# Two RMS-norm roots between two fused blocks, moved from full-width rows to token columns

## The reference, cut to what matters

```
x1  = x + (1 + gt2) * conv_ffn(h, w_up, conv_w, conv_b, w_down)    # end of the first block
y   = x1 * rsqrt(mean(x1^2) + 1e-6) * g_final                      # its final norm
hn  = y  * rsqrt(mean(y^2)  + 1e-5) * norm_mix_g_2                 # first norm of the second block
u   = hn @ w_pw1 + b_pw1                                           # 2048 -> 4096
a, gate = split(u);  u = a * sigmoid(gate)                         # then a depthwise convolution of 31 taps
```

## Time and profile before

| | us |
|---|---|
| median of 3 runs | 2610.44 |
| lowest and highest of them | 2610.17, 2610.95 |
| the profiled execution, its own time | 2608.42 |
| the span of its instructions | 2606.3 |
| busy in it: PE, DVE, ACT, POOL | 2560.7, 1837.3, 1355.5, 290.4 |
| mean granted clock of TensorE, share of full speed | 0.991 |

### The profile page before, as it was taken

The page is one execution under the profiler, slowest core; times in us unless marked ns, Lnnn a source line. Parts: engine busy times, 40 slices in busy tenths (PEclk is TensorE's granted clock), DMA queues, the critical chain, the costliest instruction groups (busy, mean ns, idle before and its releaser), DMA issues. The chain is left out here.

```text
span 2606.3 us, 42280 instructions
## 1 busy us (share of the span) xinstructions
PE 2560.7 (98%) x15879; PEld 2265.6 (87%) x15879; DVE 1837.3 (70%) x2514; ACT 1355.5 (52%) x1868; POOL 290.4 (11%) x278
## 2 busy tenths in 40 slices
PE   7999999999999999999999999999999999999998
PEld 4899998888888888888888889997888888888887
DVE  3467778887888888855666657998776654566554
ACT  3445444455645555544555556997544434444443
POOL 0021122101010000000000005881000000000000
PEclk8999999999999999999999999998999999999999
DMA  9997699867786877765666565654566655666554
GB/s 367 360 306 247 205 272 295 252 203 245 234 267 213 254 245 248 236 191 187 191 187 188 191 193 147 183 174 126 180 192 187 190 190 187 190 188 189 188 185 133
DMA packets 525083, 560.68 MB, mean 215 GB/s; under 512 B 20453, under 2 KB 487841, under 8 KB 524688
## 3 DMA queue, kind: packets, MB, share of 16 engines
q1 hardware_dynamic: 504448, 487.39, 59.2%
q0 software_dynamic: 20496, 71.38, 9.0%
HBM read 553.45 MB, written 2.10 MB: 213 GB/s over the span
## 5 line engine op out<-in xcount | busy, mean ns | idle before, releaser
L836 ACT CAST whi<-raw 128x1024 fp32r<-128x1024 f32 x850 | 890.4, 1050 | 1079.8 <-PE ps L2173 905.5
L1340 DVE TENSOR_TENSOR wlo<-raw,whi 128x1024 fp32r<-128x1024 f32 x794 | 970.8, 1224 | 675.5 <-ACT whi L836 669.1
L2171 PE MATMUL ps<-xhl,whi 128*128 128x512 f32 x3584 | 1130.5, 397 | 2.1 <-DVE xhl L1418 1.8
L2173 PEld LDWEIGHTS ps<-xhl,wlo 128*128 128x128 f32 x3584 | 674.4, 188 | 159.5
L2173 PE MATMUL ps<-xhl,wlo 128*128 128x256 f32 x3584 | 705.2, 278 | 0.0
L2171 PEld LDWEIGHTS ps<-xhl,whi 128*128 128x128 f32 x3584 | 546.9, 189 | 5.5 <-issue 4.8
L2171 PE MATMUL ps<-ghl,whi 128*128 128x512 f32 x1024 | 319.5, 393 | 0.0
L2173 PEld LDWEIGHTS ps<-ghl,wlo 128*128 128x128 f32 x1024 | 192.2, 188 | 44.5
L2171 PE MATMUL ps<-fhl,whi 128*128 128x512 f32 x704 | 219.3, 392 | 0.0
L2173 PE MATMUL ps<-ghl,wlo 128*128 128x256 f32 x1024 | 202.9, 279 | 0.0
L2173 PEld LDWEIGHTS ps<-fhl,wlo 128*128 128x128 f32 x704 | 132.1, 188 | 30.6
(11 more groups left out here) (364 smaller groups left out, 2515.9 us busy)
## 6 DMA issues: line engine op xcount, KB each, us to landing
raw<-in_w_in SPq DMA_DIRECT2D x176, 512.0 KB, 4.8
raw<-in_w_up SPq DMA_DIRECT2D x176, 512.0 KB, 3.7
raw<-in_ffn_w_up SPq DMA_DIRECT2D x128, 512.0 KB, 3.7
raw<-in_ffn_w_down SPq DMA_DIRECT2D x128, 512.0 KB, 3.5
ada<-in_w_ada POOLq DMA_DIRECT2D x106, 512.0 KB, 5.0
raw<-in_w_down SPq DMA_DIRECT2D x88, 512.0 KB, 3.5
att<-in_w_ada SPq DMA_DIRECT2D x32, 1024.0 KB, 11.0
raw<-in_conv_w_pw SPq DMA_DIRECT2D x120, 256.0 KB, 3.3
```

Source lines behind the costliest of these rows:

```text
L836: nc.scalar.copy(whi[t % SPL][:, :, :], raw[t % RAW][:, :, :]).then_inc(s_hi, 1)
L1340: nc.vector.tensor_tensor(wlo[t % SPL][:, :, :], raw[t % RAW][:, :, :], whi[t % SPL][:, :, :].bitcast(F32), ALU.subtract).then_inc(s_lo, 1)
L2171: mm(o[:, m, :, :], whi[t % SPL][:, c, m * P:(m + 1) * P], x, start=first and c == 0, stop=last and c == KC - 1, skip_group_check=True)
L2173: ins = mm(o[:, m, 0, :], wlo[t % SPL][:, c, m * P:(m + 1) * P], x[:, 0, :], start=False, stop=last and c == KC - 1, skip_group_check=True)
```

## The change

The sums of squares at the seam are taken as token columns (`row_sums`), those of x1 behind the second quarter of chunk 0 as before, those of x1 * g_final behind the first products of the third quarter, into `bank_m`. DVE makes both roots on two columns, with tokens on partitions, and puts r1 and r1 * r2 on diagonals (`nwt`, `odd`). Behind the first products of the fourth quarter PE spreads them: r1 * r2 into `bank_z`, r1 and again r1 * r2 into `bank_f`. `gained_normed` reads the spread roots from `bank_z`; ACT copies the two halves of `bank_f` into `rstd` and `rstd_first`, for which `rooted` waits.

```diff
@@ ACT
             down(1)
-            root(2)
-            root(3)
-
+            root(2, slice(0, 2))
+            root(3, slice(2, 4))
+            act.wait_ge(s_statspread, 2)
+            nc.scalar.copy(rstd[:, :], bank_f[:, T:2 * T]).then_inc(s_statrows, 1)
+            nc.scalar.copy(rstd_first[:, :], bank_f[:, 0:T]).then_inc(s_statrows, 1)
@@ DVE
-            root(2, EPS1, s_var2, 3)
-            sv.did(nc.vector.tensor_copy(rstd_first[:, :], rstd[:, :]))
+            def newton(at, spare):
+
+                r, v, w = (x[:, i:i + 2] for x, i in ((rstd, at), (varr, at), (varr, spare)))
+                sv.did(nc.vector.reciprocal(r, r))
+                sv.wait()
+                sv.did(nc.vector.tensor_tensor(w, r, r, ALU.mult))
+                sv.wait()
+                sv.did(nc.vector.scalar_tensor_tensor(w, w, -0.5, v, ALU.mult, ALU.mult))
+                sv.wait()
+                sv.did(nc.vector.scalar_tensor_tensor(r, w, 1.5, r, ALU.add, ALU.mult))
+                sv.wait()
+
+            def on_diagonal(dst, roots):
+
+                for h in range(2):
+                    nc.vector.tensor_scalar(dst[:, P * h:P * (h + 1)], ident, roots[:, h:h + 1], None, ALU.mult).then_inc(s_lndiag, 1)
+
+            first_root, second_root, both = rstd[:, 0:2], rstd[:, 2:4], varr[:, 10:12]
+            squared, gained_mean = varr[:, 6:8], varr[:, 8:10]
+            dve.wait_ge(s_var2, 3)
+            nc.vector.tensor_scalar(varr[:, 0:2], bank_o[:, 0:2], 1.0 / D, EPS1, ALU.mult, ALU.add).then_inc(s_var, 1)
+            dve.wait_ge(s_std, 3)
+            newton(0, 4)
+            sv.did(nc.vector.tensor_tensor(squared, first_root, first_root, ALU.mult))
             sv.wait()
-            root(3, EPS2, s_var2, 4, bank_f[:, 0:T], rstd_first[:, :])
-            sv.did(nc.vector.tensor_tensor(rstd[:, :], rstd[:, :], rstd_first[:, :], ALU.mult))
+            dve.wait_ge(s_var2, 4)
+            sv.did(nc.vector.tensor_tensor(gained_mean, bank_m[:, 0:2], squared, ALU.mult))
             sv.wait()
+            nc.vector.tensor_scalar(varr[:, 2:4], gained_mean, 1.0 / D, EPS2, ALU.mult, ALU.add).then_inc(s_var, 1)
+            on_diagonal(nwt, first_root)
+            dve.wait_ge(s_std, 4)
+            newton(2, 12)
+            sv.did(nc.vector.tensor_tensor(both, first_root, second_root, ALU.mult))
+            sv.wait()
+            on_diagonal(odd, both)
@@ rooted, gained_normed
+                dve.wait_ge(s_statrows, 2)
...
-                nc.vector.tensor_tensor(xtmp[:, q % 2, :, :], xraw[:, 4 * q:4 * q + 4, :], rstd.unsqueeze(1).to_broadcast([P, 4, T]),
+                nc.vector.tensor_tensor(xtmp[:, q % 2, :, :], xraw[:, 4 * q:4 * q + 4, :], bank_z[:, 0:T].unsqueeze(1).to_broadcast([P, 4, T]),
...
             dve.wait_ge(s_used, SPL + T_PW1)
+            dve.wait_ge(s_statspread, 1)
             gained_normed(0)
@@ PE
             def second_block_statistics():
 
-                older_sum(2)
-                newest_sum(2)
+                pe.wait_ge(s_old, 6 * 3)
+                for m in range(2):
+                    row_sums(older, m, m == 0, False)
+                pe.wait_ge(s_new, 8 * 3)
+                for m in range(2):
+                    ins = row_sums(newest, m, False, m == 1)
+                ins.then_inc(s_var2, 1)
+
+            def second_block_gained_statistics():
+
+                pe.wait_ge(s_oldg, 6)
+                for m in range(2):
+                    row_sums(older_g, m, m == 0, False, bank_m)
                 pe.wait_ge(s_newg, 8)
-                pe.wait_ge(s_oldg, 6)
-                for i, x in enumerate((older_g, newest_g)):
-                    for m in range(2):
-                        ins = mm(bank_f[:, 0:T], ones[:, :], x[:, m, :], start=i + m == 0, stop=i + m == 2)
+                for m in range(2):
+                    ins = row_sums(newest_g, m, False, m == 1, bank_m)
                 ins.then_inc(s_var2, 1)
+
+            def second_block_roots():
+
+                pe.wait_ge(s_lndiag, 4)
+                for rows, at, roots in ((bank_z, 0, odd), (bank_f, 0, nwt), (bank_f, T, odd)):
+                    for h in range(2):
+                        first = at + P * h
+                        ins = mm(rows[:, first:first + P], ones[:, :], roots[:, P * h:P * (h + 1)], start=first == 0, stop=True, skip_group_check=True)
+                    if rows is bank_z or at:
+                        ins.then_inc(s_statspread, 1)
@@ full (chunk 0)
                 for i in range(KC):
                     k = KC * q + i
+                    if first and q == 2 and i == 1:
+                        second_block_gained_statistics()
+                    if first and q == 3 and i == 1:
+                        second_block_roots()
```

More of the change, by code:

```diff
@@ L422, in build @@
         s_rspread = sem("roots_spread")
+        s_statspread = sem("second_block_roots_spread")
+        s_statrows = sem("second_block_root_rows_copied")
         s_std = sem("root_made")
@@ L1365, in add_older_gained, with root @@
                     nc.vector.tensor_tensor(older_g[:, :, :], older_g[:, :, :], newest_g[:, :, :], ALU.add).then_inc(s_oldg, 1)
-            def root(n, eps, ready, used, var=bank_o[:, 0:T], after=None):
+            def root(n, eps, ready, used, var=bank_o[:, 0:T]):
                 dve.wait_ge(ready, used)
[L1371 to L1376, removed]
                 nc.vector.tensor_scalar(varr[:, :], var, 1.0 / D, eps, ALU.mult, ALU.add).then_inc(s_var, 1)
@@ L2223, in one_bank_products, with row_sums @@
                 ins.then_inc(s_used, 1)
-            def row_sums(x, m, first, last):
+            def row_sums(x, m, first, last, bank=bank_o):
                 for h in range(2):
-                    ins = mm(bank_o[:, h:h + 1], x[:, m, P * h:P * (h + 1)], ones[:, 0:1], start=first and h == 0, stop=last, skip_group_check=True)
+                    ins = mm(bank[:, h:h + 1], x[:, m, P * h:P * (h + 1)], ones[:, 0:1], start=first and h == 0, stop=last, skip_group_check=True)
                 return ins
@@ L2606, in _ @@
             token_columns(2, newest[:, 1, :], last=True).then_inc(s_cvar, 1)
-            pe.wait_ge(s_lndiag, 2)
+            pe.wait_ge(s_lndiag, 6)
             for h in range(2):
```

## The result

The changed kernel takes 2614.87 us (median of 15 runs, 2612.5 to 2617.08) against 2610.53 us (15 runs, 2608.6 to 2613.36) for the kernel before: ratio 1.0015, with a 95% interval of 1.0008 to 1.0022. So it is 4.3 us slower, 0.17%: within the 0.2% that the forecast gave 0.93, but 3.6 us over the forecast of 2611.3, 0.27 us above the top of its range (as ratios, 1.0015 measured and 1.0016 for the top, 2614.6 / 2610.44), and inside the 2614.6 to 2618.1 us of rival (a). The profiled execution of after is 2616.1 us.

A forecast was written before the change was run, and what follows sets the result against it. PE was taken as the bound, busy 98% of the span. Added PE work of 1.28 us less the 0.45 us stall gave +0.83 us on 2610.44: 2611.3 us, range 2609.5 to 2614.6.

The forecast's parts named there:

- rival (a): In the seam between the blocks, two runs of one-column products lower TensorE's clock: 2614.6 to 2618.1 us, chance 0.18.
- the assumption that the clock holds: In the seam, TensorE keeps its full clock through both one-column runs, so no time is added for it.
- The sum on PE: In the seam, one-column sums 3.40 plus spread 1.33 less removed column sums 3.45: +1.28 us, bounds 1.1 to 2.7.
- Rival (b): Small products in the seam cost by their columns, so PE gains 2.1 us: 2609.9 us; chance 0.12, shared with another rival.
- The stall: PE's 0.45 us wait for POOL's late low part of the weights, in the third chunk, disappears.
- Net at the stall point: Where PE waited for POOL's low part, added PE work 1.28 less the 0.45 us stall: +0.83 us.
- The diagonals: Before the spread, DVE has the root diagonals ready 1.0 us before PE asks, so PE's wait is zero.
- rival (d): Root diagonals reach PE late, from slower steps between engines; 1 us beyond the slack gives 2612.3 us; chance 0.08.
- DVE, ACT and POOL: Quads can be normed 3.3 us earlier, but ACT's copies and table load leave POOL's start only 0.5 us earlier.
- The reach: With no other PE wait to the layer's end, the 0.83 us shift carries through to the total.

The follow-up runs named there:

- Experiments 2 and 3: Changed kernel with its one-column sums four records at a time, as one burst, or as two bursts three product steps apart: 2612.17, 2612.54, 2612.50 us.
- sums in turn: Changed kernel with the one-column sums four records at a time between product steps, spread one step earlier: 2612.17 us, 1.0006 of the kernel before.
- quads ahead: The sums in turn kernel with ACT's wait and two root copies moved behind the second quad's high part: 2612.82 us, 1.0007 of the kernel before.
- bursts apart: Changed kernel with three product steps between the two bursts instead of one, spread one step later: 2612.50 us, 1.0005 of the kernel before.

## Why the prediction was wrong in one step and right in the others

**The step that failed** is the assumption that the clock holds, which carried the forecast's 0.62; with it fell the sentence against rival (a), "there is no idle time beside them, and dense products between and behind them". Both facts were true and neither kept the clock: it fell during the second burst and stayed at 1.2 GHz through dense products with no gap. Experiments 2 and 3 show it as cause: the same records, arranged otherwise, leave the clock alone and take 3.34 us off. By the medians it is 2.05 to 3.32 us. That 3.34 us is also the lower end of rival (a)'s price, 3.3, is luck: the prediction took that from 6.56 us of work in a low stretch of 10.2 us, and the stretch here was 6.83 us long and full of work. And the time stands at the edge of the range only because the range took in this end of rival (a); the sum behind 2611.3 had no term for it.

The Trainium skill (TensorE: Matmul & The Clock Gate, section Why this matters for your kernels) has the clock drop for idle gaps between bursts. By that rule the clock would have held; the trace differs, with PE busy for 6.90 of 6.90 us at 0.51, and the trace decides. The prediction had seen the rule broken at 815 us, and let its reason weigh all the same.

**The sum on PE, +1.28 us**, measured +1.46 in three kernels with the full clock (sums in turn, quads ahead, bursts apart). The terms are right: a run of 16 one-column records 1.71 (1.70 forecast; 1574.20 to 1575.91), the spread 1.34 (1.33; 1585.43 to 1586.77). What was missing is the way back from small records to wide ones. With the bursts apart, 12 wide records behind a burst take 2.67 us (1575.70 to 1578.37) and not 12 x 0.216 = 2.59: 0.08 each time, after two bursts 0.16 of the missing 0.18. Rival (b) is out: a record costs 0.11 us with one column as with 128, and sums and spread together 3.41 + 1.34 = 4.75 us with the bursts apart. By the Trainium skill's list (same page, section Back-to-back issue gap) they would be 1.5, the prediction's estimate from that list, and a third of what was measured.

**The stall, -0.45 us**: gone, as forecast. Net at the stall point +1.00 for a forecast of +0.83, and with the clock +4.34.

**The diagonals**: no wait, so rival (d) is out. From the sums' arrival at 1579.63 the chain took 2.12 us to the end of the second pair, 1581.75 (2.30 forecast). PE asked at 1585.43, late through the low clock; without that, with the bursts apart, it took them without a gap too.

**DVE, ACT and POOL**: the source in PSUM costs the same (2.35 us for two quads; 2.36 from SBUF), the two copies take 0.66 together, to the table load (0.85 forecast), DVE waits 2.56 us for ACT's high part (2.7 forecast), and POOL's first low is at 28.45 us, less 3.34 for the clock 25.11, against 25.61 before: the 0.5 us of the forecast.

**The reach**: the shift arrives whole behind the layer, and PE's list has no wait up to there. The total of the medians, +4.34 us, is the stall point's; that they agree to the second digit is luck, given an interval of 1.8 us to either side. With that interval 4.3 us can be told from no change, where the prediction held 5.2 to be needed.

## What to carry to other kernels

Replacing wide products by many narrow ones does not save TensorE's time in proportion to the columns: here 1, 128 and 256 columns of an unsplit fp32 product cost 0.11, 0.11 and 0.22 us a record, so count records first, and let an idle VectorE add partial sums before TensorE sums over partitions (here 2.82 us at the stall point for 12 records fewer). Narrow products in bursts can cost TensorE its clock even between dense products, and in this kernel it stayed low after they ended; try them a few at a time among full-width ones, and look at the granted clock of that stretch. A low clock seen elsewhere in the same profile after the same form of instruction was better evidence here than a plausible reason why it should not happen.

## What the runs showed of the hardware

The granted clock fell in a stretch for which the profile shows PE busy throughout, and what it did depended on the order of the same records: 32 one-column records in a row 3.41 us at 0.50, two runs of 16 with 0.94 us of wide products between 6.83 us, with 2.67 us between, or four at a time, none. The 6.83 us were seen in two executions, the 3.41 us in one. Why the split pair cost twice what the single burst did is not shown; nor is how far the moment at which a burst comes, and not only its form, decides.

The clock also falls elsewhere, and not in the same way in every execution. In the profile of after there is such a stretch in the first block, which that of before does not have:

```profile
632.10:635.60 3.50, 1.50 (x13) 1.25 (x11) 2.67 (x4) 2.83 (x4) 0.70 (x1) 1.00 0.81 237
635.60:639.00 3.40, 3.40 (x11) 2.92 (x12) 0.73 (x2) 1.13 (x2) 0.02 (x1) 0.50 1.03 345
```

Here PE had been busy for only 1.50 of 3.50 us before. Five of the eight experiments have this stretch (3.4 us long, once 6.8) and three have not, and the low stretch in the later norm, 13.7 us before, was 10.2, 13.7 or 17.1 us long. The profiled execution of after is 7.7 us above that of before, where the medians differ by 4.3: its seam begins 1.98 us later already, and in its later norm the stretch is 17.1 us long, not 13.7. The scatter of some 2 us between executions may come in part from such stretches: of the 72 executions of the kernel before that ran beside the experiments, the 12 with a mean granted clock of 0.989 took 2612.0 us on average, the 45 with 0.990 took 2610.8. It was not tested further.
